# Two-block network on one core: three-pass input products of the second block, the last expert tile's second matrix in freed buffers, and the two norms between the blocks taken as one

## The reference, cut to what matters

```python
# end of block one: the experts' sum is added, then the block's last norm
y = moe(hl2, router_w, router_b, moe_w1, moe_w3, moe_w2)   # 16 experts, 2 per token
xl = xl + g2_l * y
x = rmsnorm(xl, final_g)              # x * rsqrt(mean(x*x) + EPS) * final_g
# start of block two
h = rms_norm(x, norm_gain)            # the second norm, of the first one's result
proj = einsum('bsd,de->bse', h, w_in) # 1024 -> 4352 columns
q, k, v, z_attn, u_ssm, z_ssm, g = split(proj)
attn = windowed_gqa(q, k, v, ...) * silu(z_attn)
y = s5_bidirectional(u_ssm, ...); y = gelu(y); y = y * sigmoid(y @ w_glu + b_glu)
ssm = y * silu(z_ssm)
merged = sigmoid(g_attn) * (attn @ w_branch_attn) + sigmoid(g_ssm) * (ssm @ w_branch_ssm)
x = x + merged @ w_out                # and a last norm
```

## Time and profile before

| | |
|---|---|
| time, median of 3 runs | 1509.98 us (1508.19 to 1512.98) |
| the profiled execution | 1511.27 us, its span 1509.4 us |
| busy: PE / DVE / ACT / POOL | 1313.2 / 823.2 / 556.1 / 144.3 us |
| mean granted TensorE clock | 0.921 of full |
| from the last expert tile's second product to the first square sum | 945.2 to 978.2 us |
| from the first square sum to the first input product | 978.2 to 1013.5 us |
| input products | 1013.5 to 1140.5 us |
| from there to the first gate chunk | 1140.5 to 1168.9 us |

### The profile page before, as it was taken

One profiled execution on the slowest core, in us unless ns is written; L12 is line 12 of the kernel. 1 busy time (PEld: TensorE's weight loads), 2 busy tenths in 40 slices (PEclk: granted clock), 3 DMA queues, 4 the chain that ended last, 5 costly groups with the idle time before them and its releaser, 6 DMA issues.

```text
span 1509.4 us, 16627 instructions
## 1 busy us (share of the span) xinstructions
PE 1313.2 (87%) x6328; PEld 903.7 (60%) x6328; DVE 823.2 (55%) x1221; ACT 556.1 (37%) x729; POOL 144.3 (10%) x136
## 2 busy tenths in 40 slices
PE   6999999988898976489999998559995999898796
PEld 2544465857677436378888886325443777674674
DVE  2248878558663034288888887450004566634353
ACT  1431000315444021277777776120104334425322
POOL 1100101000122000212222221200000000000000
PEclk7899999999998985699999999579998999999898
DMA  9525646390400041379999997531223455535201
GB/s 370 207 78 194 245 194 253 103 213 5 161 18 1 1 170 56 137 292 403 409 411 398 403 413 275 192 163 56 86 57 119 133 159 155 152 119 203 96 17 56
DMA packets 53108, 270.61 MB, mean 179 GB/s; under 512 B 15287, under 2 KB 22359, under 8 KB 38328
## 3 DMA queue, kind: packets, MB, share of 16 engines
q1 hardware_dynamic: 38264, 209.46, 37.8%
q0 software_dynamic: 10032, 47.21, 8.5%
q10 hardware_dynamic: 4752, 13.11, 2.2%
HBM read 229.38 MB, written 36.72 MB: 176 GB/s over the span
## 4 chain that ended last, share of the span: by engine, by line
PE 74%; DVE 12%; ACT 5%; DMA 4%; issue 3%; POOL 1%; SPq 0%; DVEq 0%; POOLq 0%; ACTq 0%
PE PS L2462 36%; PE PS L2817 6%; PE PS L2818 6%; PE PS L2819 6%; PE PS L3015 3%; PE PS L3016 3%; PE PS L3017 3%; PE PS L2895 2%; PE PS L2725 1%; PE PS L2479 1%; PE PS L2811 1%; PE PS L3001 1%; DMA ring<-in_slabs 1%; DVE rstd L1626 1%; DMA gate_scratch<-arena 1%
## 5 line engine op out<-in xcount | busy, mean ns | idle before, releaser
L2462 PE MATMUL PS<-hT,ring 128*128 128x512 f32 (+1 forms) x704 | 294.4, 578 | 11.7 <-DVE hT L2191 10.3
L2462 PEld LDWEIGHTS PS<-hT,ring 128*128 128x128 f32 x704 | 134.0, 192 | 169.1 <-issue 152.5
L2462 PE MATMUL PS<-arena 128*128 128x64 f32 (+7 forms) x776 | 191.2, 412 | 22.3 <-DMA arena<-in_small_f_w 7.8
L1293 ACT ACTIVATE arena_r<-ring 128x2048 fp32r<-128x2048 f32 x102 | 189.3, 1910 | 11.2 <-ACT arena L1303 8.8
L2462 PEld LDWEIGHTS PS<-arena 128*128 128x128 f32 (+2 forms) x776 | 118.0, 200 | 86.6 <-issue 61.6
L2129 DVE TENSOR_TENSOR arena_r<-ring,arena_r 128x2048 fp32r<-128x2048 f32 x68 | 152.7, 2287 | 13.6 <-ACT arena_r L1293 13.5
L3015 PE MATMUL PS<-arena_r 128*128 128x512 f32 x256 | 106.2, 415 | 26.3 <-DVE ring_r L2320 21.3
L2817 PE MATMUL PS<-arena_r,hT_r 128*128 128x512 f32 x272 | 112.4, 413 | 10.8 <-DVE arena_r L2129 10.8
L1134 ACT ACTIVATE arena<-PS 128x1024 f32<-128x1024 f32 (+1 forms) x32 | 30.9, 970 | 217.1 <-PE PS L2462 213.7
L2818 PE MATMUL PS<-arena_r,hT_r 128*128 128x512 f32 x272 | 108.7, 400 | 0.0
L3017 PE MATMUL PS<-arena_r,ring_r 128*128 128x512 f32 x256 | 103.1, 403 | 0.0
(11 more groups left out here) (385 smaller groups left out, 2030.3 us busy)
## 6 DMA issues: line engine op xcount, KB each, us to landing
ring<-in_moe SPq DMA_DIRECT2D x51, 2048.0 KB, 10.2
ring<-in_slabs SPq DMA_DIRECT2D x27, 2048.0 KB, 10.8
ring<-in_slabs SPq DMA_DIRECT2D x9, 1024.0 KB, 5.9
y_rows<-arena ACTq DMA_DIRECT2D x17, 512.0 KB, 9.8
ssm_scratch<-arena POOLq DMA_DIRECT2D x4, 1152.0 KB, 6.3
arena<-ssm_scratch POOLq DMA_DIRECT2D x4, 1152.0 KB, 8.1
arena<-in_tab_fwd SPq DMA_DIRECT2D x2, 2048.0 KB, 15.1
ssm_scratch<-arena POOLq DMA_DIRECT2D x4, 1024.0 KB, 10.8
```

The costliest lines, as they stand in the source:

```text
L1293: nc.scalar.activation(rounded(moe_w_hi[n][:, cols]), ring[:, n, cols], ACT.Copy).then_inc(s_moe_hi[n], 1)
L2462: ins = nc.tensor.matmul(out, lhsT, rhs, start=(n == 0), stop=(n == len(pairs) - 1))
```

## The change

1. **The last tile's w2** no longer waits for slot 2. SP loads it into slot 0 once the last w1 is split, and its high and low parts go where the last w1's stood. The first three `in2` slabs are loaded as slots 1, 2 and 0 come free, ahead of the gathers.
2. **One norm for two.** With s the squares of x, PE computes from one set of squares both the sum of x*x and the sum of x*x*final_g*final_g: it takes the square chunks as the 128x128 weights and a 128x2 matrix `gsq` (ones, final_g squared) as the moving side, 32 narrow products. The results lie with positions on partitions (four columns each); root and reciprocal act on 128x8. To bring them back, DVE multiplies the identity by them (`diag`, twice 128x512) and PE multiplies ones by `diag`, once for each norm (units n4 and nx). `hT` is then x times final_g*norm_gain times n4, read from PSUM. The first norm's result, `xT`, which only the end of the kernel needs, is formed later, behind the first unit (`normed_x`).
3. **Three-pass input products.** `h_hi` and the rest of `hT` are formed here, and each of the 18 chunks of weights is split by ACT (`in2_high`) and DVE (`in2_low`, in place) through three rounded buffers `in_hi`; the first three chunks are split ahead of the expert sum. The first unit goes through all its high by high passes, then weight rest, then `hT` rest; the others take the three passes k by k. v is computed like the others and turned by four transposes (unit v_tr). 18 chunks of 8 full products become 18 chunks of 24 passes.
4. **The rounds.** `h_high` and `h_low` are gone from rounds 0 to 2, and the gate chunks move: the first from round 3 to round 2, the next three to rounds 4, 5 and 6; round 27 has none. Some arena regions move.

```diff
-GATE_AT = {i: n for n, i in enumerate((3, 5, 6, 10, 12, 13, 17, 19, 20, 24, 26, 27, 28, 29, 30, 31))}
+GATE_AT = {i: n for n, i in enumerate((2, 4, 5, 6, 10, 12, 13, 17, 19, 20, 24, 26, 28, 29, 30, 31))}
...
@@ block.sync @@
-            load_w2(tiles - 1)
+            last = expert_of(tiles - 1)
+            sp.wait_ge(s_moe_lo[0], 2 * tiles)
+            sp.dma_start(ring[:, 0], moe_d[bass.ds(3 * last + 2, 1)].rearrange("a p c -> p (a c)")).then_inc(s_moe_w[0], 16)
+            sp.wait_ge(s_moe_lo[1], 2 * tiles)
+            load(N_BEFORE_MOE)
+            sp.wait_ge(s_moe_lo[2], 2 * tiles - 2)
+            load(N_BEFORE_MOE + 1)
+            sp.wait_ge(s_moe_lo[2], 2 * tiles)
+            load(N_BEFORE_MOE + 2)
             sp.wait_ge(s_moe_y, tiles)
-            sp.wait_ge(s_back[QT - 1], 16 * PICKS)
-            for n in range(N_BEFORE_MOE, N_BEFORE_MOE + 5):
+            for n in range(N_BEFORE_MOE + 3, N_BEFORE_MOE + 5):
                 load(n)
...
@@ block.scalar @@
+            act.wait_ge(s_moe_w[0], 16 * tiles + 16)
+            act.wait_ge(s_w1x, tiles)
+            for c in range(2):
+...
             moe_y_out(tiles - 2)
             gT_high(tiles - 1)
-            moe_high(2, tiles - 1)
             moe_y_out(tiles - 1)
...
+            for i, key in enumerate(IN2_UNITS):
+                in2_high(2 * i + 3)
+                in2_unit(key)
+                in2_high(2 * i + 4)
+            act.wait_ge(s_uscr, 16)
...
-                    if round_ < 3:
-                        for k in ((0, 1, 2), (3, 4, 5), (6, 7))[round_]:
-                            h_high(k)
-                    if round_ == 2:
+                    if round_ == 1:
                         high(0)
...
@@ block.vector @@
-            norm(("n3",), T)
-            inverse(5, rstd[:, 0:T])
+            for half in range(2):
+                key, tiles_of = ("n3", half), slice(2 * half, 2 * half + 2)
+                filled(dve, key)
+                sums = PS[:, 2 * U.slot(key):2 * U.slot(key) + 2, 0:2]
+                then(nc.vector.tensor_scalar(nst[:, 1, tiles_of], sums[:, :, 0], 1.0 / D, EPS, ALU.mult, ALU.add))
+                nc.vector.scalar_tensor_tensor(out=nst[:, 0, tiles_of], in0=nst[:, 1, tiles_of], scalar=EPS * D,
+                                               in1=sums[:, :, 1], op0=ALU.mult, op1=ALU.add).then_inc(s_dve_read, 1)
+                read(dve, key)
+            nc.vector.tensor_scalar(nst[:, 0], nst[:, 0], 1.0 / D, None, ALU.mult).then_inc(s_mean, 1)
+            inverse(5, nst[:])
+            for n in range(2):
+                nc.vector.tensor_tensor(diag[:, n], ident[:, None, :].broadcast_to([P, QT, P]),
+                                        nst[:, n, :, None].broadcast_to([P, QT, P]), ALU.mult).then_inc(s_diag, 1)
...
+            for i, key in enumerate(IN2_UNITS):
+                in2_low(2 * i + 3)
+                in2_low(2 * i + 4)
+                if i == 0:
+                    normed_x()
...
@@ block.tensor @@
-            square_sums(("n3",), sq, 3 * KD)
-            square_sums(("n4",), sq, 4 * KD)
+            for k in range(KD):
+                pe.wait_ge(s_sq, 3 * KD + k + 1)
+                for t in range(QT):
+                    ins = nc.tensor.matmul(bank(("n3", t // 2), t % 2)[:, 0:2], sq[:, k, P * t:P * t + P], gsq[:, k],
+                                           start=(k == 0), stop=(k == KD - 1))
...
+                for c in range(2):
+                    n = 2 * i + c
+                    pe.wait_ge(s_in_lo, n + 1)
+                    w = in2_weights(n)
+                    for k in range(KD):
+                        w_h, x_h = rounded(in_hi[n % 3][:, k]), rounded(h_hi[:, k])
+                        nc.tensor.matmul(bank(key, c), w_h, x_h, start=(k == 0), stop=False)
+                        nc.tensor.matmul(bank(key, c), w_h, rounded(hT[:, k, 0:T]), start=False, stop=False)
+                        ins = nc.tensor.matmul(bank(key, c), rounded(w[:, k]), x_h, start=False, stop=(k == KD - 1))
```

229 lines of the change are left out of this document (150 added, 79 removed).

## The result

The changed kernel takes 1467.03 us, median of 4 runs (1460.69 to 1469.48); the kernel before, run beside it, 1509.09 us (1507.9 to 1512.98). The ratio is 0.9714, 95% interval 0.9684 to 0.9744. That is faster, inside the range of 1443 to 1473, and 10 us above the 1457 that was forecast. The profiled execution took 1465.06 us, span 1463.2.

A forecast was written before the change was run, and what follows sets the result against it. The prediction took chain latency across PE, DVE and ACT to bound the seam, and PE's passes the products. Gains of 5.0 + 16.2 + 23.2 + 9.0 = 53.4 from 1511.3 gave 1457.9, about 1457 as median; range 1443 to 1473.

The forecast's parts named there:

- 1, the last tile's w2: End of the expert part: loading the last w2 earlier into slot 0 gains 5.0 us, bounds 0 and 7.5.
- late by ten: Last tile: lower bound, 0 us gained if the store that the last copy waits for lands ten us late.
- 2, the norms: Seam ahead of the input products: one norm for two takes 19.2 us instead of 35.4, 16.2 gained.
- 3, the products: Input products: three passes instead of full products take 103.8 us instead of 127.0, 23.2 gained.
- named as a sign: Input products: each chunk of weights was to take 5.6 to 5.8 us in the profile.
- 4, the rounds: Start of the rounds: roundings of h removed and gates moved, 9.0 us gained, bounds 0 and 12.
- a round without cover: Rounds: 1.5 us taken off the gain for a round without cover.
- the rounds give nothing: Rival for the rounds: attention's chain on DVE or sy's transfers set the pace as before, 9 us more, 1466; chance 0.12.
- the forecast's own 1449 to 1466: Whole kernel: the range of the main forecast without its rivals; chance 0.69.
- The narrow sums at full clock: Rival for the norms: the narrow sums run at full clock, 6.5 us less and up to 1.7 more, 1449; chance 0.09.
- The split sets the pace: Rival for the products: each chunk waits for its own rounding and rest, 36 us more, 1493; chance 0.08.
- The clock stays at 0.50 in the products: Rival for the products: the clock does not rise, 84 us more, 1541, slower than before; chance 0.02.

The follow-up runs named there:

- slabs_late: The changed kernel with the second and third slab of in2 loaded only when the last gather has landed: 1465.25 us, ratio 0.9691.
- w2_slot2: The changed kernel with the last w2 loaded into slot 2 again, slabs still early: 1477.27 us, ratio 0.9769.
- best: The changed kernel with the earlier kernel's gate rounds, two in2 slabs loaded late and the norm sums' second bank pair claimed later: 1460.92 us, ratio 0.9679.
- before_shift: The kernel before with the three small new buffers reserved but unused, later buffers 128 bytes higher: 1511.3 us, ratio 1.0007.
- after_same: The changed kernel run once more, unchanged: 1469.3 us, ratio 0.971.
- parts_1_2: The changed kernel with full input products again, and h_hi, h_lo and the gates in the earlier kernel's rounds: 1499.51 us, ratio 0.9889.
- gate_old: The changed kernel with the gates at the rounds where the kernel before had them: 1463.28 us, ratio 0.9656.
- after_end: The changed kernel with the three small new buffers reserved behind arena, so old buffers keep their earlier addresses: 1468.3 us, ratio 0.9718.
- after: The changed kernel itself in its first measurement and profile: median 1467.03 us, ratio 0.9714, profiled execution 1465.06 us.
- before_gate27: The kernel before with the gate of round 27 moved to round 25: 1511.34 us, ratio 0.9985.
- warm: The changed kernel with gates at rounds 20 and 27, none at 19, and eight extra full products while PE waits for the gathers: 1466.43 us, ratio 0.9696.

## Why the prediction was right, point by point

**What bounds the kernel: right.** The seam is a chain of latencies, and each cut in it arrived nearly in full behind the first square sum; the products are PE alone. One link is missing in the forecast's chain of three engines: from the copy of the last but one tile to the first sum PE's bracket names DVE, but DVE waits there for the stores and gathers, 27.5 us before and 23.5 after.

**1, the last tile's w2, -5.0: 3.9, the size was off by 1.1.** `expert_out` started 3.1 us behind the earlier copy, 4.6 sooner, as worked out, and by ScalarE's timeline the store was late next, as said. It took 10.8 us, where 3.6 to 6.8 had been taken from the earlier trace rows: 4 to 7 late, and short of the lower bound's "late by ten". slabs_late showed the cause, the slabs that stream beside it, and that it costs only 1.7 us at this place, since PE is not ready much earlier: its 24 passes took 7.4 us, between the 5.5 and 8.4 of the forecast. How much the early w2 is worth depends on what else streams: with it undone and the slabs still early, w2_slot2 lost 8.0 us in the same stretch.

**2, the norms, -16.2: 15.8 by the same marks.** The narrow burst took 13.79 us against 13.8, the chain and the wide product until the first pass 5.7 against 5.4. The earlier trace rows were the right rows: PE was busy throughout at 0.50. The Trainium skill, page "TensorE: Matmul & The Clock Gate", section "Why this matters for your kernels", advises to keep TensorE busy for the full clock, and to warm up with matmuls before a measurement; by that the burst would take 7.3 us here, an estimate. The trace disagrees: the burst stayed at 0.50 with PE busy for all of it, 13.79 us, and in slabs_late the clock fell from 1.00 to 0.50 inside the burst. But the step left out a wait: the sums take two units instead of one, so the first narrow product also waits for the second pair of transposed banks to be read, 5.9 us instead of 4.4 from the last gathered sum. best takes it back. The gain is also measured against one execution: in before_shift, whose first square sums ran faster, the same stretch of the old kernel was 32.4 us and not 35.4, which leaves 12.8.

**3, the products, -23.2: 24.8.** First unit 12.7 us to 1013.3 against 12.8; 16 chunks and the transposes 89.5 against 91.0, so a chunk took 5.56 us, just below the 5.6 to 5.8 that had been named as a sign. A pass took (89.55 - 0.6)/384 = 0.2316 us, between the 0.215 of a full product's pass and the 0.240 of the earlier trace rows; 0.235 had been chosen. By the Trainium skill, page "FP8 and Floating Point Precision", section "TensorE Precision Notes", three passes of four would have made 95.2 us of the 127.0, an estimate; the trace says 102.2. A product of three passes costs 0.695 against 0.860, 81% and not 75%. No wait closed the loop of the splits.

**4, the rounds, -9.0: 8.5 in the profiled execution, 1.5 in after_same.** That 8.5 is so near is in part luck. sv was to come at +10.4 instead of +12.0, but came at +11.9. The three roundings were gone from ScalarE, but its load of a function table, which before ran while it waited for VectorE, now stands behind that wait; before, then after:

```profile
1141.56 1.28 ACT L1475 ACT_TABLE_LOAD   x1
```

```profile
1105.52 1.28 ACT L1525 ACT_TABLE_LOAD   x1 [1.61 <-DVE stat L2325]
```

The first exponential ends its wait 4.1 us behind the products instead of 2.8, which takes back 1.3 of the 1.6 us; the load stands there in parts_1_2 and gate_old too, so it comes with neither the three passes nor the gates; whether ScalarE's new wait for `u_scr` ahead of the rounds does it was not tested. The first gate came at +19.9 for +17.6 and sy at +51.0 for +48.9, so only 2.7 us earlier than before and not 4.8. With one gate fewer behind it (5.7) that makes 8.4, and the 1.5 that had been taken off for a round without cover did not show: two misses that cancel. gate_old showed that the moved gates have hardly a part in it, 1.0 us; the rest comes with the `h_high` and `h_low` that left the rounds, and parts_1_2, which has them back in the rounds together with the full products, needs 371.0 us from the products to the end, no less than the kernel before (368.9). What no step had was the drop of the clock in a sy: 7.0 us in after_same, in an engine that is busy all the time. With it the time came out where the rival "the rounds give nothing" had put it (1466), above the forecast's own 1449 to 1466, but not by that rival's mechanism: no transfer and no chain on VectorE was in the way.

**The sum.** Of the forecast's 53.4, 46.2 were seen span against span, 7.2 less: 4.9 from the part ahead of the change, 1.1 from part 1, 1.9 from the sums and the second unit, 0.4 from the norms, and 1.1 came back in the products and rounds (33.3 for 32.2). Without the 4.9, which no run shows to be an effect of the change, 51.1. The medians differ by 42. The drop, in five of the eight profiles of such kernels, is a likely part of the rest, but this is not shown: how often an execution without a profile has it was not measured, and the profiled execution of after_end has it and is still the fastest of its six (1460.65), since its start was 11 us earlier. The profile of after alone, which has none, would have hidden it.

**The rivals.** The narrow sums at full clock: refuted, here and in slabs_late. The split sets the pace: refuted, PE had no idle gap between 1000.58 and 1102.78. The clock stays at 0.50 in the products: refuted, 1.00 from 1013.3 on.

## What to carry to other kernels

Before a term is booked as gained, look at what streams beside the transfers that the new chain waits for: the same 512 KB store took 2.7 us alone and 6.2 to 10.9 beside 2 MB loads, and moving loads earlier moved them onto it. A stretch of narrow products can lose half the clock in one execution and not in the next with the same program, so a single profile may hide 7 us: compare two profiles of the same kernel by marks before a difference is laid to the change. And a norm's sums need not go through wide products and 128x512 roots: 32 narrow ones and two diagonals, once for both norms, saved 16 us even at half clock (13 beside the fastest profile of the old kernel).

## What the runs showed of the hardware that was not expected

The granted clock fell from 1.00 to 0.50 (from 2.4 to 1.2 GHz) while PE was busy, in a run of 128x64 and 64x64 products and the gate behind it (after_same 1281 to 1295 at 0.52); with the same program it didn't fall in after. In slabs_late it fell from 1.00 to 0.50 inside the burst of 128x2 products, PE busy. In warm eight wide products raised it to 1.00, and it was back at 0.50 at the end of the wait of 3.79 us behind them. The clock in the windows and the durations do not always agree near the start: in before_gate27 the windows from 24 to 38 us say 1.00, and the sixteen products of 64x512 there take 14.02 us, twice the 7.13 of after_end. And a shift of every buffer by 128 bytes had no measurable effect (ratio 1.0007).
